# Expert weights of a mixed attention and mixture-of-experts network: transfers of two blocks instead of one, in the same six raw places

## What is computed

```python
D_MODEL, SEQ, D_FF, N_EXPERTS, TOP_K = 1024, 256, 3584, 8, 2

def swiglu(h, w_gate, w_up, w_down):
    return (jax.nn.silu(h @ w_gate) * (h @ w_up)) @ w_down

def moe_swiglu(h, w_router, w_gate, w_up, w_down):
    ht = h.reshape(B * T, D)
    logits = (ht @ w_router).astype(jnp.float32)
    top_logits, top_idx = lax.top_k(logits, TOP_K)
    top_w = jax.nn.softmax(top_logits, axis=-1)
    combine = jnp.sum(jax.nn.one_hot(top_idx, N_EXPERTS, dtype=jnp.float32) * top_w[..., None], axis=1)
    out = jnp.zeros_like(ht)
    for e in range(N_EXPERTS):
        y = swiglu(ht, w_gate[e], w_up[e], w_down[e])
        out = out + combine[:, e:e + 1].astype(ht.dtype) * y
    return out.reshape(B, T, D)
```

## Time and profile before

| | us |
|---|---|
| median of 3 runs | 1451.35 |
| lowest, highest | 1449.78, 1451.54 |
| the profiled execution's own time | 1450.19 |
| its span, first to last instruction | 1448.5 |
| PE busy | 1409.9 (97%) |
| DVE busy | 1193.8 (82%) |
| ACT busy | 974.0 (67%) |
| bytes moved | 454.36 MB, mean 314 GB/s |
| transfers of expert weights | 336 of 1024 KB |

### The profile page before, as it was taken

How to read it: one execution, slowest core, us unless ns; L and a number is a source line. 1 busy time by engine, 2 the same in 40 slices (tenths; PEclk the granted TensorE clock), 3 DMA queues, 4 the chain that set the end, 5 groups by cost and what they waited for, 6 DMA issues and landing times.

```text
span 1448.5 us, 21105 instructions
## 1 busy us (share of the span) xinstructions
PE 1409.9 (97%) x7930; PEld 1172.9 (81%) x7930; DVE 1193.8 (82%) x994; ACT 974.0 (67%) x826; POOL 161.2 (11%) x178
## 2 busy tenths in 40 slices
PE   9999999999999999999999999999999999999896
PEld 7788888888998888888888887788887788887675
DVE  7765555555987467888999998999999999999998
ACT  6544434345645535777878878888878888879785
POOL 1002000002233214860000000000000000000100
PEclk9999999999999999999999999999999999999999
DMA  9339855555431134999999999999999999999994
GB/s 367 119 117 373 325 181 192 185 176 174 146 118 60 47 125 165 384 415 388 419 418 419 413 417 391 426 425 408 419 414 373 426 425 417 414 416 413 425 427 184
DMA packets 91190, 454.36 MB, mean 314 GB/s; under 512 B 8048, under 2 KB 8560, under 8 KB 48112
## 3 DMA queue, kind: packets, MB, share of 16 engines
q1 hardware_dynamic: 84272, 431.11, 75.0%
q0 software_dynamic: 5696, 20.45, 3.6%
q10 hardware_dynamic: 1152, 1.83, 0.4%
HBM read 437.63 MB, written 15.73 MB: 313 GB/s over the span
## 4 chain that ended last, share of the span: by engine, by line
PE 81%; DVE 10%; DMA 4%; ACT 2%; issue 2%; POOL 1%; SPq 0%; DVEq 0%; ACTq 0%; POOLq 0%
PE PS L410 20%; PE PS L412 19%; PE PS L411 19%; DVE w_low L402 6%; PE PS L2264 4%; PE PS L2265 4%; DMA w_raw<-in_m_w_blocks 3%; PE PS L1837 2%; PE PS L2282 2%; PE PS L2283 2%; PE PS L2271 2%; ACT w_high L397 1%; DVE w_low_moe L402 1%; DMA w_raw<-in_a_w_qkv 1%; PE PS L1565 1%
## 5 line engine op out<-in xcount | busy, mean ns | idle before, releaser
L402 DVE TENSOR_TENSOR w_low<-w_raw,w_high 128x2048 fp32r<-128x2048 f32 x252 | 569.1, 2285 | 16.6 <-ACT w_high L397 14.5
L397 ACT ACTIVATE w_high<-w_raw 128x2048 fp32r<-128x2048 f32 x252 | 477.8, 1916 | 54.2 <-PE PS L412 35.6
L410 PE MATMUL PS<-w_high,x_high 128*128 128x512 f32 x704 | 281.5, 400 | 2.5 <-DVE x_low L2728 1.1
L412 PE MATMUL PS<-w_high,x_low 128*128 128x512 f32 x704 | 275.6, 392 | 0.0
L411 PE MATMUL PS<-w_low,x_high 128*128 128x512 f32 x704 | 274.9, 390 | 0.0
L380 DVE TENSOR_TENSOR w_low<-w_raw,w_high 128x2048 fp32r<-128x2048 f32 x69 | 158.9, 2305 | 88.1 <-ACT w_high L376 88.0
L376 ACT ACTIVATE w_high<-w_raw 128x2048 fp32r<-128x2048 f32 x69 | 132.4, 1918 | 120.1 <-PE PS L412 116.0
L402 DVE TENSOR_TENSOR w_low_moe<-w_raw,w_high_moe 128x2048 fp32r<-128x2048 f32 x84 | 192.1, 2287 | 1.1 <-ACT w_high_moe L397 0.9
L397 ACT ACTIVATE w_high_moe<-w_raw 128x2048 fp32r<-128x2048 f32 x84 | 161.7, 1925 | 21.5 <-PE PS L412 16.6
L410 PEld LDWEIGHTS PS<-w_high,x_high 128*128 128x128 f32 x704 | 132.6, 188 | 31.1 <-DVE x_low L2728 1.3
L412 PEld LDWEIGHTS PS<-w_high,x_low 128*128 128x128 f32 x704 | 132.5, 188 | 29.3
(11 more groups left out here) (416 smaller groups left out, 2295.3 us busy)
## 6 DMA issues: line engine op xcount, KB each, us to landing
w_raw<-in_m_w_blocks SPq DMA_DIRECT2D x336, 1024.0 KB, 7.8
w_raw<-in_b_w_in SPq DMA_DIRECT2D x16, 1024.0 KB, 5.1
w_raw<-in_f_w_gate SPq DMA_DIRECT2D x14, 1024.0 KB, 5.2
w_raw<-in_f_w_up SPq DMA_DIRECT2D x14, 1024.0 KB, 5.0
w_raw<-in_f_w_down SPq DMA_DIRECT2D x14, 1024.0 KB, 4.9
x_slots_dram<-zeros POOLq DMA_DIRECT2D x12, 512.0 KB, 11.5
w_raw<-in_a_w_qkv SPq DMA_DIRECT2D x5, 1024.0 KB, 14.4
w_raw<-in_a_w_o SPq DMA_DIRECT2D x4, 1024.0 KB, 15.9
```

What stands on the lines that cost most here:

```text
L397: nc.scalar.activation(ring(n, par)[0], W[:, n % RAW, :], ACT.Copy).then_inc(hi_done, 1)
L402: nc.vector.tensor_tensor(low, W[:, n % RAW, :], high.bitcast(f32), ALU.subtract).then_inc(lo_done, 1)
L410: nc.tensor.matmul(o, sH, mH, start=first, stop=False)
L412: return nc.tensor.matmul(o, sL, mH, start=False, stop=last)
```

## The change

SP fetches two blocks at once. The host puts the two blocks side by side (for each partition 16 KB in a row), a transfer is 2 MB into two neighbouring places, (0, 1), (2, 3) or (4, 5), and counts on the semaphore of the even one. SP waits for `lo_done` of the second of the two blocks that lay there; ACT waits for the even place's semaphore for either block. Nothing else changes: the same bytes, the same six places, the same conversions and matmuls in the same order. The other stages keep their blocks of 1 MB.

```diff
@@ ring_high (ACT) @@
-            act.wait_ge(w_in[n % RAW], 16 * (n // RAW + 1) + q * 16)
+            act.wait_ge(w_in[n % RAW - n % 2], 16 * (n // RAW + 1) + q * 16)
@@ the expert stage (SP) @@
-                def fetch_block(n, r, m):
-                    if n >= RAW:
-                        sp.wait_ge(lo_done, n - RAW + 1 + r * RAW)
-                    sp.dma_start(W[:, n % RAW, :], m_w_blocks[m] if isinstance(m, int) else m_w_blocks[ds(m, 1)].rearrange("a p c -> p (a c)"))\
-                        .then_inc(w_in[n % RAW], 16)
+                def fetch_two(n, r, m):
+                    if n + 1 >= RAW:
+                        sp.wait_ge(lo_done, n + 1 - RAW + 1 + r * RAW)
+                    s = n % RAW
+                    sp.dma_start(W[:, s:s + 2, :].rearrange("p r c -> p (r c)"),
+                                 m_w_blocks[m] if isinstance(m, int) else m_w_blocks[ds(m, 1)].rearrange("a p c -> p (a c)"))\
+                        .then_inc(w_in[s], 16)
...
                 def in_and_out(q, m_in, m_out):
-                    for k in range(4):
-                        fetch_block(n0 + 4 + k, q, m_in + k)
-                    for k in range(2):
-                        fetch_block(n0 + 8 + k, q, m_out + 10 + k)
+                    for k in range(2):
+                        fetch_two(n0 + 4 + 2 * k, q, m_in + k)
+                    fetch_two(n0 + 8, q, m_out + 5)
@@ expert_blocks (host) @@
-    return blocks.reshape(6 * (E * NC + 1), 128, SUB)
+    return np.ascontiguousarray(blocks.reshape(3 * (E * NC + 1), 2, 128, SUB).transpose(0, 2, 1, 3)).reshape(3 * (E * NC + 1), 128, 2 * SUB)
```

More of the change, by code:

```diff
@@ L35 @@
 SUBS_FFN = 6 * NC
+TWOS = 3 * NC
 JOBS = 11
@@ L484, in job @@
                 def job(j, e):
-                    for k in range(4):
-                        fetch_block(n0 + k, j * NC, e * SUBS_FFN + k)
+                    for k in range(2):
+                        fetch_two(n0 + 2 * k, j * NC, e * TWOS + k)
                     with sp.Fori(0, NC - 1) as i:
-                        for k in range(6):
-                            fetch_block(n0 + 4 + k, j * NC + i, e * SUBS_FFN + 6 * i + 6 + k)
+                        for k in range(3):
+                            fetch_two(n0 + 4 + 2 * k, j * NC + i, e * TWOS + 3 * i + 3 + k)
@@ L490, in job, with in_and_out @@
+                    fetch_two(n0 + SUBS_FFN - 2, j * NC, e * TWOS + TWOS + 2)
+                def in_and_out(q, m_in, m_out):
                     for k in range(2):
-                        fetch_block(n0 + SUBS_FFN - 2 + k, j * NC, e * SUBS_FFN + SUBS_FFN + 4 + k)
-                def in_and_out(q, m_in, m_out):
-                    for k in range(4):
-                        fetch_block(n0 + 4 + k, q, m_in + k)
-                    for k in range(2):
-                        fetch_block(n0 + 8 + k, q, m_out + 10 + k)
+                        fetch_two(n0 + 4 + 2 * k, q, m_in + k)
+                    fetch_two(n0 + 8, q, m_out + 5)
@@ L499, in expert_at @@
                 def expert_at(p):
                     return sp.value_load(order[0:1, p:p + 1], min_val=0, max_val=E - 1)
-                for k in range(4):
-                    fetch_block(n0 + k, 0, k)
+                for k in range(2):
+                    fetch_two(n0 + 2 * k, 0, k)
                 with sp.Fori(0, NC - 1) as q:
-                    in_and_out(q, 6 * q + 6, 6 * q)
+                    in_and_out(q, 3 * q + 3, 3 * q)
                 sp.wait_ge(sem("jobs_done"), 1)
                 wide = expert_at(1)
-                in_and_out(NC - 1, wide * SUBS_FFN, 6 * (NC - 1))
+                in_and_out(NC - 1, wide * TWOS, 3 * (NC - 1))
@@ L511, in _ @@
                     with sp.Fori(0, NC - 1) as i:
-                        in_and_out(q0 + 2 * i, slim * SUBS_FFN + 6 * i, wide * SUBS_FFN + 6 * i)
-                        in_and_out(q0 + 2 * i + 1, wide * SUBS_FFN + 6 * i + 6, slim * SUBS_FFN + 6 * i)
+                        in_and_out(q0 + 2 * i, slim * TWOS + 3 * i, wide * TWOS + 3 * i)
+                        in_and_out(q0 + 2 * i + 1, wide * TWOS + 3 * i + 3, slim * TWOS + 3 * i)
                     q1 = q0 + 2 * (NC - 1)
-                    in_and_out(q1, slim * SUBS_FFN + 6 * (NC - 1), wide * SUBS_FFN + 6 * (NC - 1))
+                    in_and_out(q1, slim * TWOS + 3 * (NC - 1), wide * TWOS + 3 * (NC - 1))
                     wide = expert_at(2 * p + 3)
-                    in_and_out(q1 + 1, wide * SUBS_FFN, slim * SUBS_FFN + 6 * (NC - 1))
+                    in_and_out(q1 + 1, wide * TWOS, slim * TWOS + 3 * (NC - 1))
                 wide = expert_at(LAST)
                 with sp.Fori(0, NC - 1) as i:
-                    in_and_out(LAST * NC + i, wide * SUBS_FFN + 6 * i + 6, wide * SUBS_FFN + 6 * i)
-                for k in range(2):
-                    fetch_block(n0 + 4 + k, E * NC - 1, wide * SUBS_FFN + 6 * (NC - 1) + 10 + k)
+                    in_and_out(LAST * NC + i, wide * TWOS + 3 * i + 3, wide * TWOS + 3 * i)
+                fetch_two(n0 + 4, E * NC - 1, wide * TWOS + 3 * (NC - 1) + 5)
                 sp.wait_ge(sem("jobs_done"), 2)
```

## The result

| | before | with the change |
|---|---|---|
| median, us | 1451.03 | 1532.64 |
| lowest to highest of four runs | 1449.78 to 1451.54 | 1527.52 to 1540.04 |
| span of the profiled execution | 1448.5 | 1530.0 |

The change makes the kernel slower: the ratio is 1.0571, with a 95% interval of 1.0556 to 1.0586, which is 82 us. The direction was forecast, the size was not: 1469 us was predicted, 1484 was the upper end.

What follows compares the result with a forecast made beforehand. PE was taken to pace the pairs and the DMA engines' rate to bound the narrow steps. Terms -0.4 + 13 + 2 + 1 + 1.9 = +17.5 us gave 1467.7 us profiled, 1469 median, range 1453 to 1484.

Steps and rivals of the forecast that it cites:

- What bounds the kernel before: Expert stage: PE paces the interleaved pairs, 2.53 us a block; the DMA engines' rate, 2.46 us a block, bounds the narrow steps.
- coarser places: Expert stage: each transfer waits for its place's second low part and lands both blocks together; 13 us in the pairs.
- The step that failed: Pairs: landing is the later of issue + 7.2 us and the landing before + 4.9; undisturbed turns cost nothing.
- The middle term: Interleaved pairs: reserve gone, so disturbed turns lose time; 13 us taken, between 2 and 22.
- The balance of 29.5 + 0.9 + 1.0 us: Pairs, one turn of 30.4 us: transfer bytes, disturbances and engine idle time need 31.4 us.
- The narrow steps: From 1360 us on: place cycle 13.8 or 14.9 us against 14.7 of bytes; +1 us (0 to 3) without the tail.
- the tail: End of the expert stage: both last blocks land together, last low part ends 6.5 us after landing; +1.9 us.
- The first expert: First expert, 590 to 640 us: POOL's transfers share the engines and SP's dry queue loses its turn; 2 us (0 to 5).
- Larger pieces: Where the engines bound: 16 KB pieces move 0.5% faster than 8 KB (0 to 3%); 0.4 us gained.
- the heavier one: Rival: engines wait at each turn of a place, full loss in the pairs, +32 us, 1483; chance 0.17.
- the faster one: Rival: the engines' rate decides, in the narrow steps, 3% of 71 us, 2.1 us, about 1448; chance 0.08.
- the signs: Trace: 168 transfers, 60080 packets, issue to landing least 7.1 to 7.3 us, median 8, ACT waits over a hundred us.

Runs made afterwards that it cites:

- experiment 6: Kernel before, still 336 transfers of 1 MB, but issue waits for the second low part and ACT waits for both landings: 1535.9 us, ratio 1.0603.
- 2: Kernel before with its 1 MB transfers and waits, reading blocks from the changed memory layout in pieces 16 KB apart: 1451.17 us, ratio 1.0001.
- 1: Changed kernel with its 2 MB transfers, but from blocks laid out as before, giving pieces of 8 KB: 1542.71 us, ratio 1.0629.
- experiment 7: Own kernel, network left out: 2 MB transfers in three double places, time from landing to release (hold) varied; nothing lost up to 5.8 us, 355 GB/s at 8.2.
- Experiment 4: Network left out, SP alone streams expert weights: full queues 421 to 429 GB/s with either piece; a lone 2 MB transfer takes 7.7 us.
- 8: Like experiment 7, with holds between and a fourth double place: 414 GB/s at 6.05 us in three places, full rate at 8.2 us in four.

## Why the prediction was wrong, point by point

- **What bounds the kernel before** was read right. That the loss would come from coarser places and not from the bytes or the instructions was right too, and the experiments show it: the waits alone make all of it (experiment 6), the layout none (2), and with the waits of the change shorter pieces do not help (1).
- **The step that failed** is the rule "Landing = the later of issue + 7.2 and the landing before + 4.9", that is, that the 2.3 us around a transfer's bytes are hidden once it is issued 2.3 us before the landing ahead of it. Measured, it takes 4.0 us (experiment 7). By my rule the change has 1.2 us of reserve (15.2 - 0.2 - 6.6 - 4.9 - 2.3), by the measured lead it has -0.5. From this came the statement that an undisturbed turn costs nothing. The 2.3 us were taken from one lone transfer, which says how long such a one takes and not how early the next one must stand in the queue.
- **The middle term, 13 us with 22 as its end,** measured 63. The balance of 29.5 + 0.9 + 1.0 us for a turn charged the engines with their best rate and an idle time. In fact they are idle for 3% of the time only and slow for the rest: 389 GB/s while busy, with one piece in ten over 0.8 us. I had read the 414 of the earlier trace rows as disturbances from outside that stay what they are, and not asked what the rate does when the queue is short. The uneven slices of the earlier trace rows could have been a hint; the transfers of the kernel before that had a lead of 3 to 4 us took 2.9 us from landing to landing where the others took 2.5.
- **The narrow steps** were forecast at +2.5 us in all and cost 14.7. It is the same failed step: I had 13.8 us for the round of a place against 14.7 of bytes. With a lead of 4.0 the round is 8.9 + 6.6 + 0.2 = 15.7, above the bytes. That is 1.0 us for each of seven rounds, 7 us, and 9 with the tail; the other 6 us are not accounted for. The granted clock (0.95 of full speed in this stretch, 0.97 before) can make up 2 to 3 us of PE's time at most. The tail was right: the last two blocks land at 1505.8 and the last low part ends at 1512.6, 6.8 us for the forecast 6.5.
- **The first expert** cost 3.8 us, within 0 to 5.
- **Larger pieces** move 1.2% faster in a full queue (428 to 423 GB/s), within the bounds of 0 and 3%, and it is worth nothing here.
- **Of the rivals** the heavier one named the right condition, more than 2.3 us around a transfer's bytes, but its price was capped at the disturbances, 1483 us. It lacked the case that the round of a place is longer than the turn, which has no such cap. In the faster one, 2% for 3% takes a third off its price and does not halve it.
- **Of the signs** the packets, the issues, ACT's waits (206 us for "over a hundred"), the DMA share (0.97) and the tail came as written. The least time from issue to landing did not (7.9 us for 7.1 to 7.3), nor the median (9.9 for 8). I had also written that I would be wrong if this time stayed at 9 us or more, and by that sign I was.
- **The rule of the Trainium skill,** page DMA: Bandwidth & Descriptors, about 2 us plus the bytes at 436 GB/s, stands in its section Anatomy of one DMA, as a fit for transfers that GpSimd issues, and not in section Measured, as I had put it. It gives 6.8 us for a lone 2 MB and 4.4 for 1 MB. Experiment 4 has 7.7 and 4.8 us for transfers that SP issues, so the measurement decides. The advice of section Measured, to batch to 1 MiB or more, the kernel before meets already; batching further made it 82 us slower.

## What to carry to other kernels

Before transfers are made larger in the same memory, add up the round of a place: lead, own bytes, hold and issue, and compare it with the pace of the engine that consumes; both the bytes and the hold grow with the transfer. Two coarsenings that cost 6 and 8 us alone can cost 85 together, so try them together. Take the lead from a stream in which transfers follow each other, not from a lone one, and treat a DMA engine that is busy as not yet one at its rate: read the GB/s beside the share.

## What the runs showed of the hardware

- A stream of 2 MB transfers keeps its full 427 GB/s when the next is issued 4.0 us before the landing ahead. Where the place comes free too late for that, the rate falls to 414 GB/s (hold 6.05 us, a lead of 3.7 us) and down to 355 (hold 8.2 us), with the engines still busy 94 to 100% of the time (experiments 7 and 8).
- Engines that start from idle mostly take up to 1.7 us, the longest 2.0, for a 16 KB piece that takes 0.61 us otherwise; pieces that start more than 3 us after the issue are at full rate again (experiment 4). In experiment 7 such slow pieces appear again with a short lead, although the engines are nearly always busy: one in 14 over 0.8 us at a hold of 6.75 us, one in nine at 8.2. In the changed kernel the pieces that start 1 to 3 us after an issue are a third of all and carry 69% of the excess over 611 ns. That the slow restart of single engines is what turns a short lead into a low rate is likely from this, but the traces name no engine for a piece, and no run took it apart; it stays open.
- Of the kernels that do the whole work none beats the one before. The nearest, the changed memory layout with single transfers, is the same within 0.1%.
